# Gate and up with four of eight k-pairs by seven block products in chunks 1 to 9, and the third weight sum of a block by an adding DMA

## The chip, the cores and the metric

One core of one Trainium2 chip runs the whole kernel. The metric is device time in microseconds (us). Engines: PE is TensorE (matmul), DVE is VectorE, ACT is ScalarE, POOL is GpSimd, SP is SyncE, which here only issues loads.

## The reference

One decoder layer on 256 tokens of width 2048, all in float32: a SwiGLU feed-forward (FFN), a token mixer (SSD and attention), a second FFN, each with a residual and a layer norm. The change touches the two FFNs:

```python
def swiglu(x, w_gate, w_up, w_down):        # 2048 -> 5632 -> 2048
    return (jax.nn.silu(x @ w_gate) * (x @ w_up)) @ w_down
```

## The kernel before

**Products.** Every float32 operand is split into a high part (rounded to fp32r by an ACT copy) and a low part (DVE: value minus high). One product of a 128-row tile of activations with a 128x512 tile of weights is three matmuls: high by high, high by low, low by high. The activations (`a_hi`, `a_lo`, transposed, 16 k-tiles x 256 tokens) stay in SBUF, the weights stream.

**Slabs.** SP loads the weights in slabs of 128x2x512 (512 KB: two k-tiles, 512 columns) into a ring of `LAND` = 4 buffers `land`. ACT makes `w_hi` of a slab (L1309), DVE makes `w_lo` (L1728), both rings of `SPLIT` = 4. ACT starts slab n once PE has used slab n-4 (semaphore `used`), PE starts slab n when its low part is there (`rest`), and SP reloads a `land` buffer when DVE is through with it (`rest` too). Each engine runs its own list of instructions strictly in order.

**FFN stages.** Gate and up take 11 chunks of 512 hidden columns (`up1`, `up2`), 16 slabs a chunk; down takes 2 double columns of 44 slabs (`down1`, `down2`). A chunk's accumulators fill one half of PSUM (`acc` or `spare`, by turns). A plain pair of slabs is 8 products, 24 matmuls.

**Seven products.** In chunks 1 to 9 the two slabs of a k-pair (gate and up, slabs 2b and 2b+1) that is in `SEVEN` are taken as a 2x2 block product with 7 in place of 8 products (21 matmuls), and so are the five pairs `DOWN_SEVEN` in each half of down. It needs four sums of weight tiles, g0, g1 being the gate slab's k-tiles and u0, u1 the up slab's. DVE makes them in `block_sums` (L1926): u0+u1, g0+u0 (written over u0 in `land`), g0+u0+u1, and that plus g1. The block's up slab is split by ACT only after the second sum. Three of the sums are operands of their own and are split into `t_hi` and `t_lo` (ACT L1420 and L1422, DVE L1943 and L1946), which exist once: ACT may write them again when PE has finished with those of the block before (`t_used`). It also needs sums of activations, which are made once per FFN (`s_hi`, `s_lo`, one pair of buffers for each member of `SEVEN`; `mixed_of`, `mixed_low`).

**The order on DVE** is written out by hand in `up_seven`: besides the 16 splits it has, at slab 1, `collect` (shared sums of the chunk before, out of PSUM), at slab 3 `sum_chunk`, at slab 4 `product_summed`, at slab 6 `hidden_low`, and ahead of slab 2b of a member of `SEVEN` `block_sums`. In the FFN stages POOL has only two refills of `resid` and a few small operations for the layer norms.

Of the kernel before, what the change touches and what calls it, by code (L numbers as in the profile page):

```python
# [19 lines left out]
F32 = mybir.dt.float32  # L20
# [64 lines left out]
SEVEN = (2, 4, 6)  # L85
# [187 lines left out]
def build_decoder_layer(nc, x, positions, ffn1_w_gate, ffn1_w_up, ffn1_w_down, ln1_g, ln1_b, w_in, conv_w, conv_b,  # L273
# [20 lines left out]
    with ctx:  # L294
# [6 lines left out]

        resid = sb("resid", [P, TOK, D])
# [7 lines left out]
        def placed(name, shape, dt, at):  # L310
# [40 lines left out]
        sz = sb("sz", [P, TOK, W])  # L351
        bcT = sb("bcT", [P, 2, SEQ])
        b_tok = sb("b_tok", [P, P])
        cbm = sb("cbm", [P, TOK, P])
# [23 lines left out]
        t_hi = placed("t_hi", [P, 2, W], F32R, 36 * K)  # L378
        t_hi_four = placed("t_hi_four", [P, W], F32R, 40 * K)
        t_lo = placed("t_lo", [P, 2, W], F32R, 80 * K)  # L380
        t_lo_four = placed("t_lo_four", [P, W], F32R, 84 * K)
        d_s = [(placed(f"d_hi{k}", [P, 4, P], F32R, at * K), placed(f"d_lo{k}", [P, 4, P], F32R, (at + 2) * K))
               for k, at in enumerate((88, 92, 108, 112, 116))]
        d_t_hi = placed("d_t_hi", [P, 2, W], F32R, 96 * K)
        d_t_hi_four = placed("d_t_hi_four", [P, W], F32R, 100 * K)
        d_t_lo = placed("d_t_lo", [P, 2, W], F32R, 102 * K)
        d_t_lo_four = placed("d_t_lo_four", [P, W], F32R, 106 * K)
# [32 lines left out]
        sums = sem("sums")  # L420
        t_high = sem("t_high")
# [160 lines left out]
        def _(pool):  # L582
# [146 lines left out]
            keep_stream(TOK * NC_D)  # L729
            pool.wait_ge(kept_out, 2 * 16 * NC_D)  # L730
# [4 lines left out]
            pool.dma_start(resid[:, :, 0:2 * W], kept_view[:, :, 0:2 * W]).then_inc(resid_in, 16)  # L735
            pool.wait_ge(used, slab_no("down2", 1, 2 * DOWN_ORDER[1].index(7) + 1) + 1)
# [5 lines left out]
        def _(pe):  # L742
# [132 lines left out]
            def seven_products(n, slab_at, lg, lu, rows_of, mixed, t_set, own, aux, first, last, turned=None):  # L875
# [424 lines left out]
        def _(act):  # L1300
# [163 lines left out]
            def down(f):  # L1464
                for j in range(2):
                    for l, (p, c) in enumerate(DOWN_SLABS[j]):
# [9 lines left out]
                        if s in DOWN_SEVEN and c == 1:  # L1476
                            n = down_block(f, j, DOWN_SEVEN.index(s))
                            act.wait_ge(sums, n * 4 + 2)
                            split(f"down{f}", j, l)
# [242 lines left out]
        def _(dve):  # L1722
# [203 lines left out]
            def block_sums(phase, i, l, n):  # L1926
# [616 lines left out]
```

## Time and profile before

| | |
|---|---|
| median of 3 runs | 2670.63 us (2668.64 to 2671.52) |
| the profiled execution | 2668.99 us, span 2667.4 us |
| granted TensorE clock | 0.996 of full speed |
| PE busy | 2634.5 us, 99% |
| DVE busy | 2002.6 us, 75% |
| ACT busy | 1361.7 us, 51% |
| DMA | 513.96 MB, mean 193 GB/s |

The span runs from the first to the last instruction of one execution. Busy shares are means over stages: in the chunks with seven products DVE is far above its mean share. A matmul's row is longer (0.39 us) than the distance to the next matmul, since they are pipelined; the distance is what a matmul costs.

### The profile page before, as it was taken

How to read it: one execution, taken by the hardware profiler on the slowest of the kernel's cores; microseconds unless marked ns; L12 is line 12 of the kernel's file. 1: busy time of each engine (PE TensorE's matmuls, PEld its weight loads, DVE VectorE, ACT ScalarE, POOL GpSimd, SP SyncE). 2: the span in 40 equal slices, each digit the busy share in tenths (PEclk: the TensorE clock that was granted, in tenths of full speed). 3: DMA queues.
4: the chain of work that ended last, by engine and by line, in shares of the span. 5: the costliest groups of instructions: out<-in, count | busy, mean ns of one | idle time of the engine just before them, and what ended most of it. 6: DMA issues, size and time to landing. Idle time of an engine off the chain costs nothing.

```text
span 2667.4 us, 36687 instructions
## 1 busy us (share of the span) xinstructions
PE 2634.5 (99%) x12546; PEld 2188.8 (82%) x12546; DVE 2002.6 (75%) x2410; ACT 1361.7 (51%) x1678; POOL 130.0 (5%) x170
## 2 busy tenths in 40 slices
PE   8999999999999999999999999999999999999997
PEld 7888888888787788888888888888878888888886
DVE  6999997688666665677777765444689999977986
ACT  5555555455344454566555554444355555554553
POOL 1000000000000000211111100000000000000000
PEclk9999999999999999999999999999999999999999
DMA  6666566666655546665555565667666665666664
GB/s 224 204 191 209 185 205 204 214 200 204 189 171 147 156 150 197 206 181 179 177 177 177 179 183 165 190 190 247 200 190 204 190 211 186 205 202 229 210 208 171
DMA packets 286195, 513.96 MB, mean 193 GB/s; under 512 B 19648, under 2 KB 52592, under 8 KB 284048
## 3 DMA queue, kind: packets, MB, share of 16 engines
q1 hardware_dynamic: 279552, 485.03, 57.8%
q0 software_dynamic: 4880, 25.36, 2.6%
q10 hardware_dynamic: 1664, 2.26, 0.2%
q8 instruction: 61, 1.00, 0.2%
q14 instruction: 38, 0.31, 0.0%
HBM read 506.23 MB, written 6.36 MB: 192 GB/s over the span
## 4 chain that ended last, share of the span: by engine, by line
PE 95%; DVE 3%; ACT 1%; issue 0%; DMA 0%; POOL 0%; POOLq 0%; SPq 0%; ACTq 0%; DVEq 0%
PE acc L787 13%; PE acc L789 13%; PE acc L788 13%; PE acc L853 5%; PE acc L855 5%; PE acc L854 5%; PE acc L871 4%; PE acc L872 4%; PE acc L873 4%; PE spare L871 4%; PE spare L872 4%; PE spare L873 4%; PE spare L855 3%; PE spare L854 3%; PE spare L853 3%; PE spare L756 2%
## 5 line engine op out<-in xcount | busy, mean ns | idle before, releaser
L1728 DVE TENSOR_TENSOR w_lo<-land,w_hi 128x1024 fp32r<-128x1024 f32 (+1 forms) x956 | 1149.2, 1219 | 499.4 <-ACT w_hi L1309 490.6
L1309 ACT ACTIVATE w_hi<-land 128x1024 fp32r<-128x1024 f32 (+1 forms) x956 | 976.8, 1029 | 916.9 <-PE acc L789 328.0
L787 PE MATMUL acc<-w_hi,a_hi 128*128 128x512 f32 (+1 forms) x1184 | 451.2, 381 | 2.6 <-DVE a_lo L1775 1.8
L789 PE MATMUL acc<-w_hi,a_lo 128*128 128x512 f32 (+1 forms) x1184 | 435.8, 368 | 0.0
L788 PE MATMUL acc<-w_lo,a_hi 128*128 128x512 f32 (+1 forms) x1184 | 434.4, 367 | 0.0
L787 PEld LDWEIGHTS acc<-w_hi,a_hi 128*128 128x128 f32 x1184 | 223.9, 189 | 46.8 <-issue 9.2
L789 PEld LDWEIGHTS acc<-w_hi,a_lo 128*128 128x128 f32 x1184 | 223.6, 189 | 38.2
L788 PEld LDWEIGHTS acc<-w_lo,a_hi 128*128 128x128 f32 x1184 | 224.1, 189 | 37.4 <-issue 3.6
L853 PE MATMUL acc<-w_hi,a_hi 128*128 128x512 f32 x576 | 227.7, 395 | 2.0 <-DVE a_lo L1775 1.7
L855 PE MATMUL acc<-w_hi,a_lo 128*128 128x512 f32 x576 | 225.1, 391 | 0.0
L854 PE MATMUL acc<-w_lo,a_hi 128*128 128x512 f32 x576 | 225.0, 391 | 0.0
L853 PE MATMUL spare<-w_hi,a_hi 128*128 128x512 f32 x400 | 156.6, 391 | 0.0
L855 PE MATMUL spare<-w_hi,a_lo 128*128 128x512 f32 x400 | 155.8, 389 | 0.0
L854 PE MATMUL spare<-w_lo,a_hi 128*128 128x512 f32 x400 | 155.6, 389 | 0.0
L853 PEld LDWEIGHTS acc<-w_hi,a_hi 128*128 128x128 f32 x576 | 108.8, 189 | 25.4 <-DVE a_lo L1775 2.1
L855 PEld LDWEIGHTS acc<-w_hi,a_lo 128*128 128x128 f32 x576 | 108.6, 189 | 23.0
L854 PEld LDWEIGHTS acc<-w_lo,a_hi 128*128 128x128 f32 x576 | 108.9, 189 | 21.9
L871 PE MATMUL spare<-w_hi,g_hi 128*128 128x512 f32 x292 | 114.0, 390 | 0.7 <-DVE w_lo L1728 0.7
L873 PE MATMUL spare<-w_hi,g_lo 128*128 128x512 f32 x292 | 113.6, 389 | 0.0
L872 PE MATMUL spare<-w_lo,g_hi 128*128 128x512 f32 x292 | 113.6, 389 | 0.0
L871 PE MATMUL acc<-w_hi,g_hi 128*128 128x512 f32 x292 | 113.6, 389 | 0.0
L872 PE MATMUL acc<-w_lo,g_hi 128*128 128x512 f32 x292 | 113.6, 389 | 0.0
(388 smaller groups left out, 4233.1 us busy)
## 6 DMA issues: line engine op xcount, KB each, us to landing
land<-w_in SPq DMA_DIRECT2D x232, 512.0 KB, 3.9
land<-ffn_w_gate SPq DMA_DIRECT2D x176, 512.0 KB, 3.9
land<-ffn_w_up SPq DMA_DIRECT2D x176, 512.0 KB, 4.3
land<-ffn_w_down SPq DMA_DIRECT2D x176, 512.0 KB, 4.7
land<-w_ssd_o SPq DMA_DIRECT2D x64, 512.0 KB, 4.3
land<-w_in SPq DMA_DIRECT2D x132, 128.0 KB, 2.3
land<-w_attn_o SPq DMA_DIRECT2D x32, 512.0 KB, 4.1
land<-w_out SPq DMA_DIRECT2D x32, 512.0 KB, 4.4
```

What stands on the lines that cost most here:

```text
L756: return pe.transpose(spare[0:src.shape[-1], bank, at:at + rows], src, ident[0:rows, 0:rows])
L787: pe.matmul(to, rows_hi, hi, start=first, stop=False)
L788: pe.matmul(to, rows_hi, lo, start=False, stop=False)
L789: mm = pe.matmul(to, rows_lo, hi, start=False, stop=last)
L853: pe.matmul(to, rows_hi, hi, start=first and k == 0, stop=False)
L854: pe.matmul(to, rows_hi, lo, start=False, stop=False)
L855: mm = pe.matmul(to, rows_lo, hi, start=False, stop=last and k == 1)
L871: pe.matmul(to, rows[0], block[0], start=first, stop=False)
L872: pe.matmul(to, rows[0], block[1], start=False, stop=False)
L873: return pe.matmul(to, rows[1], block[0], start=False, stop=last)
L1309: act.activation(w_hi[:, l % SPLIT, 0:deep, 0:width], land[:, l % LAND, 0:deep, 0:width], ACT.Copy).then_inc(high, 1)
L1728: dve.tensor_tensor(w_lo[:, l % SPLIT, 0:deep, 0:width], land[:, l % LAND, 0:deep, 0:width], w_hi[:, l % SPLIT, 0:deep, 0:width].bitcast(F ...
```

## The change

1. `SEVEN` becomes (2, 4, 5, 6): one more k-pair of chunks 1 to 9 of both FFNs by 7 products. Pairs 4, 5 and 6 are neighbours. A fourth pair of buffers for the mixed activations and one more mixing per FFN come with it.
2. The sum u0+u1 is no longer made by DVE. After DVE's first sum (g0+u0, which no longer goes over u0), POOL issues a DMA that reads u1 again from HBM (128x512, 256 KB) and adds it onto u0 in `land`. ACT splits the block's up slab after that has landed (semaphore `third_added`, L1469). This holds for the blocks of down too.
3. The other three sums lie side by side in `t_sums` and are split by one ACT and one DVE instruction of 128x1536 (L1451, L1969) in place of two each.
4. Order: ACT splits the three sums before the up slab, DVE likewise. PE takes the three products that need `t_hi` in the middle of the block, behind the gate slab's, and those of the up slab last. `collect` waits for the last up slab in place of `t_used`.

```diff
-SEVEN = (2, 4, 6)
+SEVEN = (2, 4, 5, 6)
...
+            def add_third(slot, n, block):
+
+                pool.wait_ge(sums, n * 3 + 1)
+                pool.dma_start(land[:, slot, 0, :], block, accum_op=ALU.add).then_inc(third_added, 16)
...
                 three(own[:, 0, :], rows_of(1, 0), block(lg, 1)).then_inc(used, 1)
+                pe.wait_ge(t_rest, n + 1)
+                three(aux[:, 1, :], mixed_rows(1), t_block(0), first, last)
+                if turned is not None:
+                    pe.wait_ge(gt_out, turned)
+                three(aux[:, 3, :], mixed_rows(2), t_block(1), first, last)
+                three(own[:, 1, :], rows_of(1, 1), t_block(2)).then_inc(t_used, 1)
                 pe.wait_ge(rest, slab_at + 2)
                 three(own[:, 2, :], mixed_rows(3), block(lu, 1))
-                three(aux[:, 1, :], mixed_rows(1), block(lu, 0), first, last).then_inc(used, 1)
-                if turned is not None:
-                    pe.wait_ge(gt_out, turned)
-                pe.wait_ge(t_rest, n * 2 + 1)
-                three(aux[:, 2, :], mixed_rows(0), t_block(0), first, last)
-                three(aux[:, 3, :], mixed_rows(2), t_block(1), first, last)
-                pe.wait_ge(t_rest, n * 2 + 2)
-                three(own[:, 1, :], rows_of(1, 1), t_block(2)).then_inc(t_used, 1)
+                three(aux[:, 2, :], mixed_rows(0), block(lu, 0), first, last).then_inc(used, 1)
...
-                act.wait_ge(sums, n * 4 + 3)
+                act.wait_ge(sums, n * 3 + 3)
                 if not is_zero(n):
                     act.wait_ge(t_used, n)
-                act.activation(hi[:, :, :], sz[:, :, :], ACT.Copy).then_inc(t_high, 1)
-                act.wait_ge(sums, n * 4 + 4)
-                act.activation(hi_four[:, :], t_four, ACT.Copy).then_inc(t_high, 1)
+                act.activation(t_of[t_set][0][:, :, :], t_sums[:, :, :], ACT.Copy).then_inc(t_high, 1)
...
+                    n = seven_block(f, i, l // 2) if l // 2 in SEVEN else None
+                    if n is not None and l % 2 == 1:
+                        act.wait_ge(third_added, n * 16 + 16)
+                    split(f"up{f}", i, l)
+                    if n is not None and l % 2 == 0:
                         t_high_parts(n, "up")
...
-                dve.tensor_tensor(sz[:, 0, :], up[:, 0, :], up[:, 1, :], ALU.add).then_inc(sums, 1)
-                dve.wait_ge(sums, n * 4 + 1)
-                dve.tensor_tensor(up[:, 0, :], gate[:, 0, :], up[:, 0, :], ALU.add).then_inc(sums, 1)
-                dve.wait_ge(sums, n * 4 + 2)
-                dve.tensor_tensor(sz[:, 1, :], up[:, 0, :], up[:, 1, :], ALU.add).then_inc(sums, 1)
-                dve.wait_ge(sums, n * 4 + 3)
+                dve.tensor_tensor(sz[:, 0, :], gate[:, 0, :], up[:, 0, :], ALU.add).then_inc(sums, 1)
+                dve.wait_ge(sums, n * 3 + 1)
+                dve.tensor_tensor(sz[:, 1, :], sz[:, 0, :], up[:, 1, :], ALU.add).then_inc(sums, 1)
+                dve.wait_ge(sums, n * 3 + 2)
                 dve.tensor_tensor(t_four, sz[:, 1, :], gate[:, 1, :], ALU.add).then_inc(sums, 1)
...
-                    split(f"up{f}", i, l)
                     if l // 2 in SEVEN and l % 2 == 1:
                         t_low_parts(seven_block(f, i, l // 2), "up")
+                    split(f"up{f}", i, l)
```

The order on DVE in chunk 1, before, from the sums of pair 4 (slabs 8 and 9) to the first sum of pair 6; `w_lo` is a slab's split (x2: two in a row), `t_lo` and `t_lo_four` those of the sums:

```order
L1931 TENSOR_TENSOR sz<-land 128x512
L1933 TENSOR_TENSOR land<-land 128x512
L1935 TENSOR_TENSOR sz<-land 128x512
L1937 TENSOR_TENSOR bcT<-sz,land 128x512
L1728 TENSOR_TENSOR w_lo<-land,w_hi 128x1024 x2
L1943 TENSOR_TENSOR t_lo<-sz,t_hi 128x1024
L1946 TENSOR_TENSOR t_lo_four<-bcT,t_hi_four 128x512
L1728 TENSOR_TENSOR w_lo<-land,w_hi 128x1024 x2
L1931 TENSOR_TENSOR sz<-land 128x512
```

The same engine and place in the changed kernel, pairs 4 and 5:

```order
L1959 TENSOR_TENSOR t_sums<-land 128x512
L1961 TENSOR_TENSOR t_sums<-t_sums,land 128x512
L1963 TENSOR_TENSOR t_sums<-t_sums,land 128x512
L1756 TENSOR_TENSOR w_lo<-land,w_hi 128x1024
L1969 TENSOR_TENSOR t_lo<-t_sums,t_hi 128x1536
L1756 TENSOR_TENSOR w_lo<-land,w_hi 128x1024
L1959 TENSOR_TENSOR t_sums<-land 128x512
L1961 TENSOR_TENSOR t_sums<-t_sums,land 128x512
L1963 TENSOR_TENSOR t_sums<-t_sums,land 128x512
L1756 TENSOR_TENSOR w_lo<-land,w_hi 128x1024
L1969 TENSOR_TENSOR t_lo<-t_sums,t_hi 128x1536
L1756 TENSOR_TENSOR w_lo<-land,w_hi 128x1024
```

One sum fewer stands ahead of a block's splits, the split of the sums has moved ahead of the up slab's, and pair 5, which had two plain splits, repeats the whole sequence directly behind pair 4.

The order on PE in chunk 1, before: the second half of pair 4's block and the plain slab behind it. Only the first of each product's three matmuls stands here:

```order
L871 MATMUL spare<-w_hi,s_hi1_84 128x512 [waits rest]
...
L871 MATMUL acc<-w_hi,s_hi1_84 128x512
...
L871 MATMUL acc<-t_hi_89,s_hi1_84 128x512 [waits t_rest]
...
L871 MATMUL acc<-t_hi_89,s_hi1_84 128x512
...
L871 MATMUL spare<-t_hi_four_90,a_hi_49 128x512 [waits t_rest]
...
L853 MATMUL spare<-w_hi,a_hi_49 128x512 [waits rest]
```

The same engine in the changed kernel, from the last `t_hi` product of pair 4 to the first of pair 5:

```order
L904 MATMUL spare<-t_hi_91,a_hi_49 128x512
...
L904 MATMUL spare<-w_hi,s_hi1_84 128x512 [waits rest]
...
L904 MATMUL acc<-w_hi,s_hi1_84 128x512
...
L904 MATMUL acc<-w_hi,a_hi_49 128x512 [waits rest]
...
L904 MATMUL spare<-w_hi,a_hi_49 128x512
...
L904 MATMUL acc<-t_hi_91,s_hi2_85 128x512 [waits t_rest]
```

Between the last use of `t_hi` in one block and its first use in the next there are now four products, twelve matmuls. Before, a plain pair and the first four products of the next block lay between, 36 matmuls.

## Rows read from the trace of the kernel before

**Rows 1.** page, part 1: busy us (share of the span) xinstructions of each engine
```profile
PE 2634.5 (99%) x12546; PEld 2188.8 (82%) x12546; DVE 2002.6 (75%) x2410; ACT 1361.7 (51%) x1678; POOL 130.0 (5%) x170
```

**Rows 2.** windows, two of up 1 and one of down 1; us, busy of PE, PEld, DVE, ACT, POOL
```profile
84.00:126.00 42.00, 42.00 (x191) 34.86 (x190) 39.09 (x43) 23.81 (x26) 0.00 (x0) 1.00 0.60 192
126.00:168.00 42.00, 42.00 (x191) 34.88 (x190) 38.46 (x42) 23.83 (x26) 0.00 (x0) 1.00 0.63 198
511.00:604.00 93.00, 93.00 (x412) 77.01 (x411) 82.35 (x98) 47.66 (x51) 0.00 (x0) 1.00 0.62 202
```

**Rows 3.** timeline, PE: the first product of a block, and of the slab behind
```profile
154.66 0.39 PE L871 MATMUL acc<-w_hi,a_hi 128*128 128x512 f32 x1
...
159.42 0.39 PE L853 MATMUL spare<-w_hi,a_hi 128*128 128x512 f32 x1
```

**Rows 4.** timeline, DVE: pair 4 of one chunk; start us, us, instruction [idle before]
```profile
158.13 0.68 DVE L1931 TENSOR_TENSOR sz<-land 128x512 f32<-128x512 f32 x1
...
160.30 0.69 DVE L1937 TENSOR_TENSOR bcT<-sz,land 128x512 f32<-128x512 f32 x1
160.91 2.35 DVE L1728 TENSOR_TENSOR w_lo<-land,w_hi 128x1024 fp32r<-128x1024 f32 x2
163.18 1.22 DVE L1943 TENSOR_TENSOR t_lo<-sz,t_hi 128x1024 fp32r<-128x1024 f32 x1
164.32 0.69 DVE L1946 TENSOR_TENSOR t_lo_four<-bcT,t_hi_four 128x512 fp32r<-128x512 f32 x1
164.92 2.46 DVE L1728 TENSOR_TENSOR w_lo<-land,w_hi 128x1024 fp32r<-128x1024 f32 x2
167.65 0.69 DVE L1931 TENSOR_TENSOR sz<-land 128x512 f32<-128x512 f32 x1 [0.27 <-DMA land<-ffn_w_up]
```

**Rows 5.** timeline, DVE: the other work of a chunk
```profile
139.72 1.22 DVE L1954 TENSOR_TENSOR resid<-spare,resid 128x1024 f32<-128x1024 f32 x1
...
143.14 1.21 DVE L1870 TENSOR_TENSOR resid<-resid,acc 128x1024 f32<-128x1024 f32 x1
...
145.60 1.22 DVE L1728 TENSOR_TENSOR w_lo<-land,w_hi 128x1024 fp32r<-128x1024 f32 x1
146.74 1.22 DVE L1877 TENSOR_TENSOR resid<-resid 128x1024 f32<-128x1024 f32 x1
147.88 0.68 DVE L1931 TENSOR_TENSOR sz<-land 128x512 f32<-128x512 f32 x1
...
154.67 1.28 DVE L1885 SCALAR_TENSOR_TENSOR g_lo<-acc,g_hi 128x512 f32 x2
155.87 2.35 DVE L1728 TENSOR_TENSOR w_lo<-land,w_hi 128x1024 fp32r<-128x1024 f32 x2
...
180.65 0.69 DVE L1952 TENSOR_TENSOR resid<-resid,acc 128x512 f32<-128x512 f32 x1 [1.71 <-ACT resid L1427]
...
182.10 1.23 DVE L1954 TENSOR_TENSOR resid<-acc,resid 128x1024 f32<-128x1024 f32 x1
```

**Rows 6.** groups of instructions, up 1, ACT: busy us, mean ns | idle before
```profile
L1309 ACT ACTIVATE w_hi<-land 128x1024 fp32r<-128x1024 f32 x129 | 137.0, 1062 | 130.1 <-DVE land L1933 53.0 <-PE spare L855 35.6 <-PE acc L855 34.5
...
L1420 ACT ACTIVATE t_hi<-sz 128x1024 fp32r<-128x1024 f32 x24 | 25.1, 1044 | 0.0
...
L1422 ACT ACTIVATE t_hi_four<-bcT 128x512 fp32r<-128x512 f32 x24 | 14.8, 615 | 0.0
```

**Rows 7.** DMA issues: KB each, median us from issue to landing
```profile
land<-ffn_w_up SPq DMA_DIRECT2D x176, 512.0 KB, 4.3
...
kept<-resid POOLq DMA_DIRECT2D x8, 512.0 KB, 3.6
...
resid<-x POOLq DMA_DIRECT2D x2, 1024.0 KB, 8.1
...
out<-resid ACTq DMA_DIRECT2D x8, 256.0 KB, 2.0
...
par<-conv_w POOLq DMA_DIRECT2D x2, 48.0 KB, 5.5
```

More of the change, by code:

```diff
@@ L349, in build_decoder_layer @@
         state = placed("state", [P, W], F32, 94 * K)
[L351 to L354, printed above, removed]
+        t_sums = sb("t_sums", [P, 3, W])
+        sz = t_sums[:, 0:TOK, :]
+        t_four = t_sums[:, TOK, :]
+        bcT = t_four.rearrange("p (k n) -> p k n", k=2)
+        group_at = -(-nc.sbuf_base // 32) * 32
+        group = sb("group", [P, 4, P])
+        b_tok = group[:, 0, :]
+        cbm = group[:, 1:1 + TOK, :]
         ident = sb("ident", [P, P])
@@ L377, in build_decoder_layer @@
         s_lo = [placed(f"s_lo{k}", [P, 4, P], F32R, at * K) for k, at in enumerate((94, 86, 42))]
[L378 to L381, printed above, removed]
+        s_hi.append(placed("s_hi3", [P, 4, P], F32R, resid_at - at0 + 8 * W))
+        s_lo.append(placed("s_lo3", [P, 4, P], F32R, group_at - at0))
+        t_hi = placed("t_hi", [P, 3, W], F32R, 36 * K)
+        t_lo = placed("t_lo", [P, 3, W], F32R, 80 * K)
         d_s = [(placed(f"d_hi{k}", [P, 4, P], F32R, at * K), placed(f"d_lo{k}", [P, 4, P], F32R, (at + 2) * K))
                for k, at in enumerate((88, 92, 108, 112, 116))]
[L384 to L387, printed above, removed]
+        d_t_hi = placed("d_t_hi", [P, 3, W], F32R, 96 * K)
+        d_t_lo = placed("d_t_lo", [P, 3, W], F32R, 102 * K)
         d_parts = placed("d_parts", [P, 3, W], F32, 120 * K)
-        t_of = {"up": (t_hi, t_hi_four, t_lo, t_lo_four),
-                "down": (d_t_hi, d_t_hi_four, d_t_lo, d_t_lo_four)}
-        t_four = bcT[:, :, :].rearrange("p k n -> p (k n)")
+        t_of = {"up": (t_hi, t_lo), "down": (d_t_hi, d_t_lo)}
         q_one = resid[:, 0, 3 * W:4 * W]
@@ L420, in build_decoder_layer @@
         sums = sem("sums")
+        third_added = sem("third_added")
         t_high = sem("t_high")
@@ L651, in refill_late, with up_thirds, chunk, down_thirds @@
                 pool.dma_start(resid[:, :, 2 * W:], view[:, :, 2 * W:]).then_inc(resid_late_in, 16)
+            def add_third(slot, n, block):
+                pool.wait_ge(sums, n * 3 + 1)
+                pool.dma_start(land[:, slot, 0, :], block, accum_op=ALU.add).then_inc(third_added, 16)
+            def up_thirds(f):
+                def chunk(i):
+                    for b in SEVEN:
+                        add_third((2 * b + 1) % LAND, seven_block(f, i, b), ffn_w[f][1][:, 2 * b + 1, bass.ds(i * W, W)])
+                for i in range(1, ALONE + 1):
+                    chunk(i)
+                with pool.Fori(1, 1 + (NC_S - ALONE) // 2) as m:
+                    for k in range(2):
+                        chunk(m * 2 + (ALONE - 1 + k))
+            def down_thirds(f):
+                for j in range(2):
+                    for l, (p, c) in enumerate(DOWN_SLABS[j]):
+                        s = DOWN_ORDER[j][p]
+                        if s in DOWN_SEVEN and c == 1:
+                            at = (2 * j + 1) * W
+                            add_third(l % LAND, down_block(f, j, DOWN_SEVEN.index(s)),
+                                      ffn_w[f][2][:, 2 * s + 1, at:at + W])
+            up_thirds(1)
             refill_late(1, x_view)
@@ L655, in _ @@
             pool.dma_start(resid[:, :, 0:2 * W], x_view[:, :, 0:2 * W]).then_inc(resid_in, 16)
+            down_thirds(1)
             deviations(1)
@@ L729, in _ @@
             keep_stream(TOK * NC_D)
+            up_thirds(2)
             pool.wait_ge(kept_out, 2 * 16 * NC_D)
@@ L883, in t_block @@
                 def t_block(m):
-                    hi, hi_four, lo, lo_four = t_of[t_set]
-                    return (hi[:, m, :], lo[:, m, :]) if m < 2 else (hi_four[:, :], lo_four[:, :])
+                    hi, lo = t_of[t_set]
+                    return hi[:, m, :], lo[:, m, :]
                 pe.wait_ge(rest, slab_at + 1)
@@ L1457, in copy_one_down @@
             def copy_one_down(f, j):
-                act.wait_ge(t_used, down_block(f, j, len(DOWN_SEVEN) - 1) + 1)
+                last = 2 * DOWN_ORDER[j].index(DOWN_SEVEN[-1]) + 1
+                act.wait_ge(used, slab_no(f"down{f}", j, last) + 1)
                 if j == 1:
@@ L1475, in down @@
                             copy_one_down(f, 1)
[L1476 to L1479, printed above, removed]
+                        n = down_block(f, j, DOWN_SEVEN.index(s)) if s in DOWN_SEVEN else None
+                        if n is not None and c == 1:
+                            act.wait_ge(third_added, n * 16 + 16)
+                        split(f"down{f}", j, l)
+                        if n is not None and c == 0:
                             t_high_parts(n, "down")
-                        else:
-                            split(f"down{f}", j, l)
             ffn(1, "xT", None)
@@ L2080, in down @@
                             block_sums(phase, j, l, n)
-                        split(phase, j, l)
                         if n is not None and c == 1:
                             t_low_parts(n, "down")
+                        split(phase, j, l)
                 evacuate_down(f, 1, 0)
```

25 lines of the change are left out of this document (9 added, 16 removed).

## The prediction

> **What bounds the kernel now.** I read the page's busy times first: PE is busy for 99% of the span [rows 1], so a change pays only where PE gets less to do and isn't made to wait. Then the windows, because DVE's 75% is a mean: in chunks of `up1` with seven products PE is busy for all of 42.00 us and DVE for 38.5 to 39.1; in `down1` DVE is busy for 82.35 of 93.00 [rows 2]. So these chunks have two engines near their limit, PE at it and DVE some 3 us behind it. The timelines give prices. From the first product of a block to the slab behind it, 21 matmuls, are 159.42 - 154.66 = 4.76 us, 0.2267 us each [rows 3]. A chunk is 182.10 - 139.72 = 42.38 us (from `collect` to `collect`) [rows 5].
>
> **What DVE does in a chunk**, by the distance from start to start, which is what an instruction costs its engine. A split of a slab: (163.18 - 160.91)/2 = 1.135. Four sums: three at (160.30 - 158.13)/3 = 0.723 and a last one at 0.61, together 2.78; the splits of the sums 1.14 + 0.60 = 1.74 [rows 4]. `sum_chunk` 145.60 - 143.14 = 2.46, `product_summed` 1.14, `hidden_low` 155.87 - 154.67 = 1.20, `collect` 182.10 - 180.65 = 1.45 and one more of 1024 elements, 1.14 [rows 5]. Before: 16 x 1.135 + 2.46 + 1.14 + 1.20 + 2.59 = 25.55, and three blocks of 4.52, 39.1 us in all.
>
> **The change, part by part.**
>
> Saved on PE: one more pair by 21 in place of 24 matmuls, 3 x 0.2267 = 0.68 us a chunk; 9 chunks in each of 2 FFNs, 18 x 0.68 = 12.2 us. That is all there is to win: the reordering inside a block takes no matmul away.
>
> DVE after: a block has three sums, 2 x 0.723 + 0.61 = 2.06, and one split of 1536 elements. Of 512 elements this kind takes 0.69 us, of 1024 1.22 [rows 4], so 1536 take 1.75, and 1.14 + 0.53 = 1.67 from start to start. 3.73 a block, four blocks 14.9: 40.5 us of work in a chunk of 41.7. It fits, but only 1.2 us is left for waits.
>
> The new wait of DVE in each block. The split of the sums now stands ahead of the up slab's, so only the gate slab's split covers ACT's work on `t_hi`. ACT takes 0.615 us for 512 and 1.044 for 1024 elements [rows 6], so 1.47 for 1536. From the start of the third sum: it ends at 0.69, ACT runs from 0.73 to 2.20, DVE could go on at 2.24 (0.04 for a signal, as between 158.13 + 0.68 and the next sum) and is there at 0.61 + 1.135 = 1.75. It waits 0.5 us, four times a chunk, 2.0. A second wait: pair 4's sums need slab 9, whose load starts when slab 5 is split. From the end of such a split to the first sum that waited for its landing are 167.65 - (160.91 + 2.35) = 4.39 us [rows 4]. Between the two DVE now has only `hidden_low` and two splits (before, the split of the sums as well): slab 5's split starts, slab 9 is there 1.22 + 4.39 = 5.6 later, DVE is there at 1.14 + 1.20 + 2.27 = 4.6. 1.0 us. DVE-paced, a chunk is then 40.5 + 2.0 + 1.0 = 43.5 us, **1.1 more than now**, if the adding DMA is never late.
>
> The new wait of PE. `t_hi` and `t_lo` exist once. Let 0 be where PE has issued the last `t_hi` product of pair 4 (its result is there at 0.16, since a row is 0.39 long [rows 3]). ACT makes pair 5's `t_hi` from 0.20 to 1.67, DVE `t_lo` from 1.71 to 3.46. PE has only 12 matmuls in between, 2.72 us, and goes on at 3.50: **0.78 us** of waiting. Its nine matmuls end at 5.54, slab 11's six at 6.90. DVE, started at 1.71, meanwhile has the split of the sums (1.67), slab 11 (1.14), three sums (2.06) and slab 12's split (1.22 to its end): 7.8. PE waits **0.93**, and its six matmuls end at 9.19. ACT begins `t_hi` of pair 6 when the sums are there, at 6.69, DVE has `t_lo` at 9.95: PE waits **0.80**. 2.5 us a chunk, so a PE-paced chunk is 42.38 - 0.68 + 2.51 = 44.2 us, **1.8 more than now**. Pairs 2 and 4 are covered by a plain pair, as all are now. Behind pair 6 six plain slabs follow, in which DVE catches up.
>
> The adding DMA, which no row of this trace shows. Call A the time from POOL's issue to its landing. Counted from the first sum's start it is issued at 0.73 and landed at 0.73 + A; ACT splits the up slab (1.06 [rows 6]), and DVE can take it at 1.87 + A. DVE's own work brings it there at 2.06 + 1.135 + 0.5 + 1.67 = 5.4. So A is free up to 3.5 us. Above that each us costs DVE 4 us a chunk. With the 0.7 by which the PE-paced chunk is longer, the run grows from A = 3.7 on, by 18 x 4 = 72 us for each us. Bounds: 2.0 us, a transfer of the same 256 KB, from another queue with no loads beside it; 8.1 us, 1024 KB on POOL's queue beside the slabs [rows 7]. Between them, on POOL's queue, 512 KB took 3.6 and the smallest 5.5, and a slab of 512 KB takes 4.3 on SP's [rows 7]. The add fetches 256 KB and must also read the 256 KB that it adds to, so I count it as 512 KB and take the middle of 3.6 and 4.3, 3.9 us.
>
> The Trainium skill (DMA: Bandwidth & Descriptors, Anatomy of one DMA, SWDGE path) fits such a transfer by 2.0 us plus 1 us for each 436,000 bytes: an estimate of 2.6 us for 256 KB, by which the add would never be late and the sum would be that of the first rival. For 512 KB it gives 3.2, below the 3.6 of POOL's row [rows 7].
>
> Queues and neighbours. POOL has nothing else in these chunks; its refills come behind the last add, and the add's wait for a sum holds back nothing that another engine wants. The loads get 1 MB a chunk more beside 8 MB. The fourth mixing (some 2.3 us of DVE in chunk 0, twice) lies in a chunk with PE nearly full and six slabs to catch up; I count it at nothing, at most 5 us. Down: a block and the plain pair behind it are 45 matmuls, 10.2 us; DVE has 3.73 + 4 x 1.135 + 0.5 = 8.8. 1.4 us is spare, so down loses nothing until A = 4.9 and gains nothing, since its matmuls stay as many.
>
> **The sum.** With A = 3.9 a chunk is DVE-paced at 43.5 + 4 x 0.4 = 45.1 us, 2.7 more than 42.38; 18 chunks, 49 us. Against the profiled execution's own 2668.99 that is 2718 us. The median of the three runs is 1.6 us above that execution, which I leave inside the rounding.
>
> **The rivals.**
> - *The add is in time* (A up to 3.7, chance 0.33). PE's three waits remain: 18 x 1.83 = 33 us, 2702. For it: 2.0 us for 256 KB, 3.6 for twice that; against it: a slab of the same traffic takes 4.3.
> - *The add is slow by nature* (A above 5.5, 0.11). At 5.5 a chunk is 51.5, 18 x 9.1 = 164 us, and 20 blocks of down lose 0.6 each: 2845. At 8.1 it is 3084. For it: the smallest transfers of POOL took 5.5, and this one reads what it writes to.
> - *PE's wait isn't there* (faster, 0.09). If ACT and DVE had the three sums' splits ready within the 12 matmuls at pairs 5 and 6, PE would keep its 0.68 us a chunk: 2657. It decides at the place of the 0.78: the two splits and three signals would have to take 2.6 us, not 3.3. For it: only that no instruction of 1536 elements stands in the trace. Against it: two sizes of each do, and they lie on a line. Waits that come to 0.68 a chunk give 2669, no change (0.04).
>
> **How the numbers follow.** The forecast, an add of 3.7 to 5.5 us that makes DVE the pace, has 0.43: from 2702 to 2845, with 2718 where the nearest rows put it. The range from 2690 to 2840 takes in the first rival with some us less waiting than worked out, and leaves out the slow add (0.11) and the two cases without loss. A measurement here can tell about 0.2%, 5.3 us, from no change: slower by more 0.87, within it 0.04, faster 0.09.
>
> **What would show it.** In the changed kernel's chunks: PE idle at L904 for 0.8 us twice and 0.9 once, released by the split of the sums (L1969) and by a slab's split (L1756); DVE idle for 0.5 us ahead of L1969, released by ACT L1451; the add's row with its landing, and ACT's L1341 waiting for it, if A is above 3.5; a chunk of 44 to 45 us. No idle PE at pairs 5 and 6 would make the prediction wrong, and so would an A far from 4.

## The result, and the profile after

| | before | changed |
|---|---|---|
| median | 2670.57 us (4 runs, 2668.64 to 2671.52) | 2831.78 us (4 runs, 2828.56 to 2836.22) |
| profiled execution, span | 2667.4 us | 2826.9 us |
| a chunk of `up1` with seven products, `collect` to `collect`, mean of 8 | 42.39 us | 50.08 us |

The ratio is 1.0606, 95% interval 1.0587 to 1.0624: 161 us slower. I had forecast slower by 49, 2690 to 2840. The time lies inside that range, near its end, but the loss is 3.3 times the one that I forecast.

The page of the changed kernel: busy times, and the chain that ended last by engine and by line.

```profile
PE 2672.9 (95%) x12492; PEld 2167.7 (77%) x12492; DVE 2028.6 (72%) x2344; ACT 1369.1 (48%) x1624; POOL 209.2 (7%) x262
...
PE 53%; DMA 23%; DVE 13%; issue 6%; ACT 4%; POOLq 0%; DVEq 0%; POOL 0%; ACTq 0%; SPq 0%
DMA land<-ffn_w_up 16%; PE acc L820 13%; PE acc L822 12%; PE acc L821 12%; DMA land<-ffn_w_down 7%; DVE w_lo L1756 5%; ACT w_hi L1341 4%; DVE t_sums L1959 2%; PE spare L789 2%; PE acc L886 2%; PE acc L888 2%; PE acc L887 2%; PE spare L1242 1%; PE acc L904 1%; PE acc L905 1%
```

PE's share fell from 99% [rows 1] to 95%, and the chain now runs for 23% of the span through DMAs, nearly all of them `land<-ffn_w_up` and `land<-ffn_w_down`. Windows of the changed kernel, two in `up1` and one in `down1` (us, then busy of PE, PEld, DVE, ACT and POOL with counts, granted clock, DMA share, GB/s):

```profile
105.00:155.00 50.00, 44.06 (x190) 34.25 (x189) 41.01 (x41) 24.54 (x24) 3.47 (x4) 1.00 0.69 190
155.00:205.00 50.00, 42.81 (x185) 33.24 (x185) 39.94 (x40) 23.90 (x24) 3.49 (x4) 1.00 0.66 183
615.00:710.00 95.00, 91.54 (x393) 72.63 (x392) 70.19 (x69) 41.30 (x40) 5.11 (x6) 1.00 0.68 204
```

PE did 191 matmuls in 42 us before [rows 2] and does 185 to 190 in 50 us now, at the same granted clock. DVE is busy for 80 to 82%, less than the 92 to 93% of before [rows 2]: it has little more to do and waits for the rest. DVE's timeline at pair 4 (start us, us, instruction, idle before it and who ended that):

```profile
174.86 0.69 DVE L1959 TENSOR_TENSOR t_sums<-land 128x512 f32<-128x512 f32 x1 [0.23 <-DMA land<-ffn_w_up]
...
176.31 0.69 DVE L1963 TENSOR_TENSOR t_sums<-t_sums,land 128x512 f32<-128x512 f32 x1
176.92 1.22 DVE L1756 TENSOR_TENSOR w_lo<-land,w_hi 128x1024 fp32r<-128x1024 f32 x1
178.56 1.76 DVE L1969 TENSOR_TENSOR t_lo<-t_sums,t_hi 128x1536 fp32r<-128x1536 f32 x1 [0.42 <-ACT t_hi L1451]
182.26 1.23 DVE L1756 TENSOR_TENSOR w_lo<-land,w_hi 128x1024 fp32r<-128x1024 f32 x1 [1.95 <-ACT w_hi L1341]
183.41 0.68 DVE L1959 TENSOR_TENSOR t_sums<-land 128x512 f32<-128x512 f32 x1
```

The splits of a slab and the sums take what they took in [rows 4], the split of 1536 elements takes 1.76 us (1.75 worked out), and DVE waits 0.42 us for `t_hi` (0.5 worked out). The next row is the loss: the up slab's split at 182.26 comes after 1.95 us of idleness. DVE could have had it at 178.56 + 1.67 = 180.2. POOL's adds, and ACT:

```profile
176.18 0.88 POOL L658 DMA_DIRECT2D land<-ffn_w_up  x1 [10.78 <-DVE t_sums L1959]
184.72 0.87 POOL L658 DMA_DIRECT2D land<-ffn_w_up  x1 [7.67 <-DVE t_sums L1959]
```

```profile
177.03 1.49 ACT L1451 ACTIVATE t_hi<-t_sums 128x1536 fp32r<-128x1536 f32 x1 [3.32 <-DVE t_sums L1963]
181.17 2.01 ACT L1341 ACTIVATE w_hi<-land 128x1024 fp32r<-128x1024 f32 x2 [2.65 <-DMA land<-ffn_w_up]
185.58 1.48 ACT L1451 ACTIVATE t_hi<-t_sums 128x1536 fp32r<-128x1536 f32 x1 [2.40 <-DVE t_sums L1963]
189.80 2.00 ACT L1341 ACTIVATE w_hi<-land 128x1024 fp32r<-128x1024 f32 x2 [2.74 <-DMA land<-ffn_w_up]
```

The first sum of pair 4 ends at 174.86 + 0.69 = 175.55. POOL begins the DMA at 176.18, 0.63 us later, and ACT can split the up slab at 181.17, 4.99 us after that. In pair 5 it is 184.72 to 189.80, 5.08. DMA issues (KB each, median us from issue to landing):

```profile
land<-ffn_w_gate SPq DMA_DIRECT2D x176, 512.0 KB, 4.7
...
land<-ffn_w_up POOLq DMA_DIRECT2D x72, 256.0 KB, 4.6
...
land<-ffn_w_down POOLq DMA_DIRECT2D x20, 256.0 KB, 4.5
```

The add takes 4.6 us to land. The slabs of gate take 4.7, which had 3.9 before; those of up, which took 4.3 [rows 7], now take 3.8. Four of PE's waits at pairs 5 and 6:

```profile
186.74 0.50 PE L904 MATMUL acc<-w_hi,a_hi 128*128 128x512 f32 x1 [1.09 <-DVE w_lo L1756]
...
188.91 0.50 PE L904 MATMUL acc<-t_hi,s_hi 128*128 128x512 f32 x1 [0.52 <-DVE t_lo L1969]
...
192.18 0.50 PE L904 MATMUL spare<-w_hi,s_hi 128*128 128x512 f32 x1 [0.94 <-DVE w_lo L1756]
...
195.37 0.50 PE L904 MATMUL acc<-w_hi,a_hi 128*128 128x512 f32 x1 [1.53 <-DVE w_lo L1756]
```

One of these waits (188.91) is the `t_lo` wait that I had worked out; the others are for a slab's split. Over the chunks of `up1` (105 to 555 us) PE waits 16 times for `t_lo`, 8.2 us together, and 32 times for a slab's split, 29.7 us: it now waits mostly for what the late add holds up. A third wait comes once a chunk, in pair 2's block (8 times, 12.1 us): there PE waits for `hidden_low`, which DVE does behind the up slab's split, and so behind the add.

### The profile page after: what moved, and what is told of

Same layout as the page of the kernel before. It is cut to its first block, busy times and chain, and to the rows that moved or that the text cites. A ratio compares the mean times of both kernels' runs of the same rounds, so it can differ in the third digit from the quotient of the medians.

```text
span 2826.9 us, 36677 instructions
## 1 busy us (share of the span) xinstructions
PE 2672.9 (95%) x12492; PEld 2167.7 (77%) x12492; DVE 2028.6 (72%) x2344; ACT 1369.1 (48%) x1624; POOL 209.2 (7%) x262
## 3 DMA queue, kind: packets, MB, share of 16 engines
q10 hardware_dynamic: 1664, 2.26, 0.2%
## 4 chain that ended last, share of the span: by engine, by line
PE 53%; DMA 23%; DVE 13%; issue 6%; ACT 4%; POOLq 0%; DVEq 0%; POOL 0%; ACTq 0%; SPq 0%
DMA land<-ffn_w_up 16%; PE acc L820 13%; PE acc L822 12%; PE acc L821 12%; DMA land<-ffn_w_down 7%; DVE w_lo L1756 5%; ACT w_hi L1341 4%; DVE t_sums L1959 2%; PE spare L789 2%; PE acc L886 2%; PE acc L888 2%; PE acc L887 2%; PE spare L1242 1%; PE acc L904 1%; PE acc L905 1%
## 5 line engine op out<-in xcount | busy, mean ns | idle before, releaser
L822 PEld LDWEIGHTS acc<-w_hi,a_lo 128*128 128x128 f32 x1184 | 223.5, 189 | 38.3
L821 PEld LDWEIGHTS acc<-w_lo,a_hi 128*128 128x128 f32 x1184 | 224.1, 189 | 37.3 <-issue 3.6
L1451 ACT ACTIVATE t_hi<-t_sums 128x1536 fp32r<-128x1536 f32 x72 | 107.1, 1487 | 211.7 <-DVE t_sums L1963 205.3
L886 PE MATMUL acc<-w_hi,a_hi 128*128 128x512 f32 x512 | 203.0, 396 | 3.8 <-DVE w_lo L1756 2.2
L887 PE MATMUL acc<-w_lo,a_hi 128*128 128x512 f32 x512 | 200.2, 391 | 0.0
L1969 DVE TENSOR_TENSOR t_lo<-t_sums,t_hi 128x1536 fp32r<-128x1536 f32 x72 | 126.6, 1759 | 31.6 <-ACT t_hi L1451 31.6
L658 POOL DMA_DIRECT2D land<-ffn_w_up x72 | 62.4, 867 | 896.2 <-DVE t_sums L1959 871.1
L886 PE MATMUL spare<-w_hi,a_hi 128*128 128x512 f32 x320 | 125.5, 392 | 0.0
L888 PE MATMUL spare<-w_hi,a_lo 128*128 128x512 f32 x320 | 124.6, 389 | 0.0
L887 PE MATMUL spare<-w_lo,a_hi 128*128 128x512 f32 x320 | 124.6, 389 | 0.0
```

Of the source, the lines that this page charges most:

```text
L821: pe.matmul(to, rows_hi, lo, start=False, stop=False)
L822: mm = pe.matmul(to, rows_lo, hi, start=False, stop=last)
L886: pe.matmul(to, rows_hi, hi, start=first and k == 0, stop=False)
L887: pe.matmul(to, rows_hi, lo, start=False, stop=False)
L888: mm = pe.matmul(to, rows_lo, hi, start=False, stop=last and k == 1)
L1451: act.activation(t_of[t_set][0][:, :, :], t_sums[:, :, :], ACT.Copy).then_inc(t_high, 1)
```

## The experiments

Eleven kernels, each an edit of the changed one. "Chunk" is the mean of eight distances from `collect` to `collect` in `up1`. "Against before" is against the kernel before as it ran beside each experiment (2669.3 to 2669.7 us). "Down" is what the two down stages lost in the profiled execution, from the last `collect` of up to the end of DVE's slabs. "Rest" is what remains of the loss after 18 x (chunk - 42.39): mostly down, and the first chunk of each FFN. It takes `up1`'s chunk for both FFNs, and in some kernels that use GpSimd the chunks of `up2` are shorter (49.55 us in the changed one, 44.66 in e1, 45.62 in e6, 45.67 in e9). Counted with them the rest is 28, 26, 17 and 16 us in these four.

| kernel | pairs | third sum | order | median us | against before | chunk us | rest us | down us |
|---|---|---|---|---|---|---|---|---|
| changed | 4 | awaited add | new | 2831.8 | +161.2 | 50.08 | 23 | 26 |
| e1_three | 3 | awaited add | new | 2739.6 | +69.9 | 44.99 | 23 | 28 |
| e2_dvesum | 4 | DVE | new | 2724.3 | +54.6 | 44.69 | 13 | 11 |
| e3_three_dvesum | 3 | DVE | new | 2681.4 | +11.7 | 42.39 | 12 | 10 |
| e4_poolsum | 4 | GpSimd | new | 2777.7 | +108.0 | 47.12 | 23 | 23 |
| e5_late | 4 | add, issued 1.45 us later | new | 2966.5 | +297.2 | 56.34 | 46 | 50 |
| e6_plain | 4 | copy, no add | new | 2748.5 | +79.2 | 46.11 | 12 | 17 |
| e7_traffic | 3 | DVE, adds to nobody | new | 2692.7 | +23.4 | 42.59 | 20 | 23 |
| e8_parts | 4 | DVE | by pair | 2722.9 | +53.6 | 45.38 | 0 | -1 |
| e9_half | 4 | half an add | new | 2747.8 | +78.5 | 46.03 | 13 | 15 |
| e10_nosum | 4 | none | new | 2718.1 | +48.8 | 44.47 | 11 | 8 |
| e11_nosum_parts | 4 | none | by pair | 2658.9 | -10.4 | 41.70 | 2 | 0 |

**e1_three**: pair 5 is taken plainly again.

```diff
-SEVEN = (2, 4, 5, 6)
+SEVEN = (2, 4, 6)
```

> The changed kernel with pair 5 taken plainly again (three pairs of seven products, as before), all else as changed: adding DMA, one split of 1536, new order. Theory (the late add paces the FFN chunks through VectorE): an add takes 0.6 us to start and 4.6 to land, 5.2 from the end of the first sum; three blocks a chunk each make VectorE wait 1.7 us and more, so a chunk is 44.3 to 46.5 us in place of 42.4 and the kernel is 40 to 80 us slower than before. Rival (the single t_hi/t_lo buffer between neighbouring pairs is what costs): no pairs are neighbours here, so it is within 10 us of before.

Ratio 1.0256 (1.0235 to 1.0276). With no neighbours in the chunk 70 us are still lost, so the add costs by itself.

**e2_dvesum**: DVE makes u0+u1, after the other three sums; no adding DMA.

```diff
...
-                        act.wait_ge(third_added, n * 16 + 16)
+                        act.wait_ge(sums, n * 4 + 4)
...
                 dve.tensor_tensor(t_four, sz[:, 1, :], gate[:, 1, :], ALU.add).then_inc(sums, 1)
+                dve.wait_ge(sums, n * 4 + 3)
+                dve.tensor_tensor(up[:, 0, :], up[:, 0, :], up[:, 1, :], ALU.add).then_inc(sums, 1)
...
```

> The changed kernel with four pairs, but the third weight sum made by VectorE again (in place, as the fourth of four sums; no adding DMA). Theory: TensorE's waits at the neighbouring pairs and VectorE's full chunk remain, 44 to 45 us a chunk: 30 to 45 us slower than before, and 115 to 130 us faster than the changed kernel. Rival (the add is everything, four pairs would win): 12 us faster than before.

Ratio 1.0205 (1.0188 to 1.0222), 107.5 us faster than the changed kernel. The chunk of 44.69 is where the theory had it; the total is 10 us above its range, and 11 are lost in down, which the theory left out.

**e3_three_dvesum**: both edits together.

> Three pairs and the third sum by VectorE, so that only the joined split of 1536 and the new order inside a block are left of the change. Theory: TensorE stays the bound, 0 us from before (within 5). Rival (the new order itself costs, since VectorE waits 0.4 us in each block for ACT's split of the sums): 5 to 30 us slower.

Ratio 1.0042 (1.0025 to 1.0059). The theory holds for the chunks, 42.39 as before, and not for the kernel: the new order costs 11.7 us, all outside them and 10 of them in down. The rival had the size, but not the place. With e1 the four kernels make a sum: order 11.7, pair 5 with the sum by DVE 42.9, the add 58.2 with three pairs and 107.5 with four.

**e4_poolsum**: GpSimd makes the sum.

```diff
-                pool.dma_start(land[:, slot, 0, :], block, accum_op=ALU.add).then_inc(third_added, 16)
+                pool.tensor_tensor(land[:, slot, 0, :], land[:, slot, 0, :], land[:, slot, 1, :], ALU.add
+                                   ).then_inc(third_added, 1)
...
```

> The changed kernel with four pairs, the third sum made by a GpSimd tensor_tensor of 128x512 in land in place of the adding DMA; ACT waits for it as it did for the DMA. A GpSimd instruction of that size takes 1.04 us in the SSD stage, so it is done long before ACT wants the up slab. Theory: only TensorE's waits at the neighbouring pairs remain, about 44.4 us a chunk: 30 to 40 us slower than before. Rival (VectorE and GpSimd hinder each other when both read SBUF): VectorE's rows of 1.22 us get longer where GpSimd runs, and it is over 60 us slower.

Ratio 1.0407 (1.0389 to 1.0424). The rival had the size, 108 us, but not the rows: DVE's splits of 1.22 us stay as they were, and one of its sums gets longer. Groups of instructions of this kernel, from 150 to 420 us (busy us, mean ns | idle before):

```profile
L658 POOL TENSOR_TENSOR land<-land 128x512 f32<-128x512 f32 x23 | 41.3, 1795 | 234.9 <-DVE t_sums L1960 234.9
...
L1964 DVE TENSOR_TENSOR t_sums<-t_sums,land 128x512 f32<-128x512 f32 x23 | 38.3, 1664 | 0.8
...
L1962 DVE TENSOR_TENSOR t_sums<-t_sums,land 128x512 f32<-128x512 f32 x23 | 15.9, 692 | 0.8
```

The third DVE sum (L1964), which runs beside GpSimd's, takes 1664 ns, and GpSimd's own takes 1795 where 1.04 us was the time of one of this size in the SSD stage. The second DVE sum (L1962, 692 ns) is no longer than before, although it starts within 0.1 us of GpSimd's row (177.40 and 177.44 in one block); rows of GpSimd are rough, and I did not settle why only the third one pays. Four times 0.97 us is 3.9 a chunk, and 43.5 + 3.9 = 47.4 (measured 47.12). The Trainium skill (SBUF — State Buffer, Who interferes with whom) has the rule: a DVE instruction with two SBUF inputs contends with a GpSimd instruction that reads SBUF. The trace agrees: 0.97 us more on DVE, 0.75 on GpSimd. So GpSimd's engine was no cheap place for a sum beside a busy DVE.

**e5_late**: the add is issued after the third sum.

```diff
-                pool.wait_ge(sums, n * 3 + 1)
+                pool.wait_ge(sums, n * 3 + 3)
```

> The changed kernel, but GpSimd issues the adding DMA after the third sum in place of the first, 1.45 us later (two sums at 0.72); nothing else moves. Theory (VectorE is paced by the add's landing, 4 times a chunk): a chunk grows by 4 x 1.45 = 5.8 us, from 49.8 to 55.6, and the kernel by 18 x 5.8 = 104 us up there plus at most 20 x 1.45 = 29 us in down: 105 to 135 us slower than the changed kernel. Rival (the add costs through the DMA traffic it makes, not through the wait): no slower than the changed kernel, within 10 us.

Ratio 1.1114 (1.1095 to 1.1132), 134.7 us slower than the changed kernel. The chunk grew by 6.26 us, 4.3 for each us of delay, where the theory had 4. Some of the difference may be TensorE's clock: in this run the granted clock was 0.87 to 0.96 over the stretches of 56 us from 108 to 556 us, where the changed kernel had 1.00, and the two chunks with 0.87 and 0.89 took 57.1 and 56.8 us, most of the others 55.8 to 56.1. Down lost 24 us more than in the changed kernel: at 6.6 us from sum to landing it is past its own spare time too.

**e6_plain**: the same DMA without the addition. The operand is u1 in place of u0+u1.

```diff
-                pool.dma_start(land[:, slot, 0, :], block, accum_op=ALU.add).then_inc(third_added, 16)
+                pool.dma_start(land[:, slot, 0, :], block).then_inc(third_added, 16)
```

> The changed kernel with the same 256 KB DMA from GpSimd's queue, without the addition: the tile u1 is copied over u0, so the output is not the reference's. It prices the addition itself. Theory: reading what it adds to is a second stream, so that without it the landing falls by the 0.4 to 1 us that I put on it, from 4.6 to about 3.8, and the kernel is 30 to 70 us faster than the changed one. Rival: fixed times of GpSimd's queue (0.6 us to start, the rest to land) make nearly all of it, and the kernel is the same within 15 us.

Ratio 1.0293 (1.0276 to 1.0310), 83 us faster than the changed kernel. Its DMA issues:

```profile
land<-ffn_w_up POOLq DMA_DIRECT2D x72, 256.0 KB, 3.7
```

0.9 us less to land, 4.0 us less of chunk. The theory had the direction and too small a size: 83 us, where it allowed 70.

**e9_half**: the add takes 256 of the 512 columns, so the sum is half made.

```diff
-                pool.dma_start(land[:, slot, 0, :], block, accum_op=ALU.add).then_inc(third_added, 16)
+                pool.dma_start(land[:, slot, 0, 0:W // 2], block[:, 0:W // 2], accum_op=ALU.add).then_inc(third_added, 16)
```

> The changed kernel, but the adding DMA takes only the first 256 of 512 columns (128 KB), so the sum is half made and the output is not the reference's. It tells size from fixed time. Theory (the landing is mostly fixed time: 4.6 us for 256 KB on GpSimd's queue, 5.5 for 48 KB at the start): landing falls by 0.5 us or less, 0 to 36 us faster than the changed kernel. Rival (bytes beside the slabs' traffic make it): landing falls by 1 us or more, over 60 us faster.

Ratio 1.0297 (1.0280 to 1.0314), 84 us faster than the changed kernel. Its DMA issues:

```profile
land<-ffn_w_up POOLq DMA_DIRECT2D x72, 128.0 KB, 3.6
```

My theory here was wrong and the rival right: half the bytes land 1.0 us earlier. Adding 128 KB (3.6 us) and copying 256 KB (3.7 us) take nearly the same.

**e7_traffic**: e3 with the same adds issued by GpSimd onto a scratch tile, and no engine of the computation waiting for them.

```diff
...
-                pool.wait_ge(sums, n * 3 + 1)
-                pool.dma_start(land[:, slot, 0, :], block, accum_op=ALU.add).then_inc(third_added, 16)
+                pool.wait_ge(sums, n * 4 + 1)
+                if not is_zero(n):
+                    pool.wait_ge(third_added, n * 16)
+                pool.dma_start(group[:, :, :].rearrange("p a n -> p (a n)"), block, accum_op=ALU.add
+                               ).then_inc(third_added, 16)
...
```

> Three pairs and the third sum by VectorE (the kernel that was 11.7 us slower than before), and GpSimd issues the same adding DMAs after the first sum, onto a scratch tile of 2 KB a partition for which no engine of the computation waits. It prices the traffic alone: 74 adds of 256 KB beside the slabs. Theory (the wait is the cost, not the traffic): within 8 us of the kernel without them, so 10 to 20 us slower than before. Rival (the adds slow down the slabs' loads and so VectorE): 30 us slower than before or more, as a good part of the 70 us of three pairs with the awaited add.

Ratio 1.0084 (1.0067 to 1.0101), 11.7 us above e3: more than the 8 that I allowed, far less than the 58.2 of the awaited add. The chunks grew by 0.2 us at most, 3 in all; down lost 23 us where e3 lost 10 (profiled executions). DVE's waits for the slabs' landing from 440 to 705 us, which is mostly `down1` (us in total, times, longest), before, in e3 and in e7:

```profile
DVE sz L1931 <- DMA land<-ffn_w_down: 2.4, 5, 0.7
```

```profile
DVE t_sums L1955 <- DMA land<-ffn_w_down: 13.2, 8, 2.9
```

```profile
DVE t_sums L1964 <- DMA land<-ffn_w_down: 22.6, 9, 4.0
```

**e10_nosum**: nobody makes the sum u0+u1; the product takes u0 alone.

```diff
...
-                        act.wait_ge(third_added, n * 16 + 16)
+                        act.wait_ge(sums, n * 3 + 1)
...
```

(The same in down, and GpSimd's calls of the add are gone.)

> The changed kernel without the sum u0+u1: no adding DMA, nobody makes the sum, ACT splits the up slab without a wait for it, so that product has the wrong operand and the output is not the reference's. This is the first rival of the prediction in pure form, an add that is never late. Theory: TensorE waits 0.8, 0.9 and 0.8 us at the neighbouring pairs, a chunk is 44.2 us, the kernel 33 us slower than before, some more with what down loses by the order (10 us, as with three pairs). Rival (the waits at the neighbours aren't there once VectorE has the time): 12 us faster than before, plus 10 of down.

Ratio 1.0183 (1.0166 to 1.0200). The theory's sum was 33 + 10, measured 48.8, and the chunk is 44.47 against 44.2. PE's waits over 270 us, some six chunks (us in total, times, longest):

```profile
PE spare L900 <- DVE t_lo L1965: 3.7, 6, 0.7
PE acc L900 <- DVE t_lo L1965: 3.7, 6, 0.7
PE spare L900 <- DVE w_lo L1752: 1.8, 3, 0.6
PE acc L900 <- DVE w_lo L1752: 1.8, 3, 0.6
```

Two waits for `t_lo` and one for a slab in each chunk, 0.6 us each, and nothing else. That idle time is 1.8 us a chunk, of the 2.8 by which the chunk is longer than e11's. A wait costs more than its idle time, as the starts show:

```profile
226.03 0.39 PE L902 MATMUL spare<-w_hi,s_lo 128*128 128x512 f32 x1
227.03 0.50 PE L900 MATMUL spare<-w_hi,a_hi 128*128 128x512 f32 x1 [0.61 <-DVE w_lo L1752]
227.36 0.39 PE L901 MATMUL spare<-w_lo,a_hi 128*128 128x512 f32 x1
```

The distance into the wait is 1.00 us in place of 0.227 and the one behind it 0.33: 0.88 us for 0.61 of idleness. The other two waits of this chunk, at 222.70 and 229.21, cost 0.99 and 0.81 in the same way, 2.7 together of the 2.8.

**e11_nosum_parts**: e10 with the parts of a block in an order that depends on the pair (g: the gate slab's products, t: those with `t_hi`, u: the up slab's); ACT and DVE split the up slab first.

```diff
+UP_PARTS = {2: "gtu", 4: "tgu", 5: "gtu", 6: "gut"}
...
+                    split(f"up{f}", i, l)
                     if l // 2 in SEVEN and l % 2 == 1:
                         t_low_parts(seven_block(f, i, l // 2), "up")
-                    split(f"up{f}", i, l)
...
```

> As the kernel without the sum u0+u1 (output not the reference's), but the order inside the blocks is chosen so that the single t_hi/t_lo buffer has time between neighbours: pair 4 takes its three t_hi products first, pair 5 in the middle, pair 6 last, 18 matmuls (4.1 us) between uses in place of 12 (2.7 us); ACT and VectorE split the up slab before the sums, as before the change, in up and in down. Theory: TensorE's waits vanish, a chunk is 41.7 to 41.9 us, the kernel 8 to 12 us faster than before. Rival (VectorE's load of four pairs is what makes TensorE wait, whatever the order): about as slow as the one with the order of the change, 30 to 45 us slower than before.

Ratio 0.9961 (0.9947 to 0.9975). Windows:

```profile
142.00:184.00 42.00, 42.00 (x191) 34.87 (x190) 40.61 (x41) 25.45 (x25) 0.00 (x0) 1.00 0.62 203
184.00:226.00 42.00, 42.00 (x191) 34.85 (x190) 40.91 (x41) 24.87 (x24) 0.00 (x0) 1.00 0.61 201
```

PE is busy for all of 42.00 us again and a chunk takes 41.70, which is 42.39 less 0.69: the three matmuls saved, at last. The same work in another order is 59 us faster than e10: 18 x 2.77 = 50 in the chunks, 9 in the rest, nearly all of it in down. The edit changed two things, the order of the parts on PE and that of the splits on ACT and DVE; I did not separate them.

**e8_parts**: e11's order, and DVE makes the sum. A complete kernel.

> Four pairs, the order with 18 matmuls between uses of t_hi, up slab split before the sums (the kernel without the sum that was 10.4 us faster than before), and now with the sum u0+u1 made by VectorE as the fourth of four: a complete kernel. Theory (VectorE's budget: 40.5 us without that sum, of a 41.8 us chunk): 4 x 0.72 more is 43.4 us, VectorE paces the chunk at 43.4 to 44.9, 18 to 45 us slower than before. Rival (the waits at the neighbours were all that four pairs cost): at least as fast as before.

Ratio 1.0201 (1.0183 to 1.0218). The chunk is 45.38, half a us above the theory's range. DVE at pairs 5 and 6:

```profile
218.11 0.69 DVE L1959 TENSOR_TENSOR t_sums<-land 128x512 f32<-128x512 f32 x1
...
220.90 2.51 DVE L1756 TENSOR_TENSOR w_lo<-land,w_hi 128x1024 fp32r<-128x1024 f32 x2
223.57 1.76 DVE L1971 TENSOR_TENSOR t_lo<-t_sums,t_hi 128x1536 fp32r<-128x1536 f32 x1 [0.16 <-ACT t_hi L1452]
225.53 0.69 DVE L1959 TENSOR_TENSOR t_sums<-land 128x512 f32<-128x512 f32 x1 [0.20 <-DVE t_lo L1971]
```

7.42 us from one block's sums to the next, where its work is 2.78 + 2.27 + 1.67 = 6.7: the last sum before the up slab's split now holds up ACT, and through it both splits. But even without that a chunk would be 43.4. This is what decides against four pairs: with the sum, DVE has more to do than a chunk of 42.39 holds. No version that I ran computes the reference in less time than the kernel before. An add that starts earlier, on a copy of u0 in a buffer of its own, was not tried.

## Why the prediction was wrong, step by step

**The saving on PE** was right: 0.68 us a chunk, and e11 shows 0.69.

**DVE's work and its wait for `t_hi`** were right: 0.41 to 0.42 us of waiting for 0.5. DVE's wait for slab 9 was too large: 1.0 us a chunk worked out, 0.4 measured (8 waits, 3.5 us, in `up1`). With both, the 43.5 us that a chunk should take with an add in time are some 0.9 too many.

**PE's waits at neighbouring pairs** were right: 2.5 us a chunk worked out, 2.35 measured in e10 (from start to start), and 0.3 more for the slower start behind each, so 44.47 - 41.70 = 2.8 between e10 and e11. The first rival, the add in time, was forecast at 2702; e10 is that case at 2718, of which 8 us were lost in down.

**The step that failed is the size of A**, "the middle of 3.6 and 4.3, 3.9 us", and with it the 0.04 us for a signal ahead of POOL's issue. The landing takes 4.6 us, and POOL begins 0.63 us after the sum that it waits for: 5.2 us from the sum, where I had 3.94. The rule around it holds. Above 3.5 us each us should cost 4 us a chunk: 43.5 + 4 x (5.2 - 3.5) = 50.3, measured 50.08; e6 with 0.9 us less gives 46.11; e5 with 1.45 us more gives 56.34. With the right size the sum would have been 18 x 7.9 = 143 us for the chunks; measured are 9 x 7.69 in `up1` and 9 x 7.16 in `up2`, 134. The agreement is in part luck, since the 43.5 is 0.9 too high and other waits in the chunk make that up. The slope is the firmer finding: 4.3 to 4.4 us a chunk for each us of path, from 4.3 to 6.6 us.

The 0.63 could have been read. In the trace before, POOL's refill waits for `sum_chunk`:

```profile
439.85 1.21 DVE L1870 TENSOR_TENSOR resid<-resid,spare 128x1024 f32<-128x1024 f32 x1
...
441.63 0.73 POOL L651 DMA_DIRECT2D resid<-x  x1 [431.20 <-DVE resid L1870]
```

The DVE row ends at 441.06 and POOL begins at 441.63, 0.57 us later. The signal was read from DVE to DVE, and this path ends at another engine. For the landing, I took the 3.6 us of `kept<-resid` as the price of 512 KB on POOL's queue. The equivalence that I used held at the one size tried, 128 KB added for 256 KB copied (e9 and e6). The row that I compared with did not: a plain copy of half its bytes, 256 KB, took 3.7 us in e6. Traffic does not explain that, since `kept<-resid` also ran beside slabs (DMA share 0.64 from 720 to 735 us, with 0.60 to 0.63 in the chunks [rows 2]). It is a store to HBM and the add a load, but no run separates the two, so why it lands sooner stays open. The nearer rows were the slabs' own, which are loads of 512 KB: 3.9 us for gate, 4.3 for up and 4.7 for down in the kernel before. The fit of the Trainium skill (DMA: Bandwidth & Descriptors, Anatomy of one DMA) gives an estimate of 2.6 us for 256 KB; the trace does not agree, since even the plain copy of e6 took 3.7 beside the slabs.

**Down** was forecast to lose nothing up to A = 4.9 and lost 26 us, counted as nothing in the sum. The runs show three parts.

- *The new order*, 8 to 11 us in down: e2, e3 and e10 lose 11, 10 and 8, while e8 and e11, with the old one, lose nothing. It is lost in `down2` (8.5 to 10.2 us); `down1` loses 0 to 2, though DVE's waits for landings there grew from 2.4 to 13.2. So those waits are mostly covered, and I had read them as the loss. PE in e3 idles for 0.6 us in all of `down1` and for 5.0 in `down2`, most of it in one place near the end:

```profile
2625.06 0.80 PE L900 MATMUL acc<-w_hi,g_hi 128*128 128x512 f32 x1 [3.48 <-DVE w_lo L1752]
```

There a slab lands late (ACT waits 5.3 us for it, while GpSimd loads `last_rows`, 2 MB), and DVE has the shared sums of `collect_down` ahead of the next four splits. e11 has no such wait of PE. Which part of the new order makes it, I did not test.

- *The adds' traffic*: e7, where nobody waits for the adds, loses 23 us in down, 13 more than e3, and `down1` then loses 12.
- *The wait for the add*, small in the changed kernel (26 against 23) and large in e5: 24 us more for 1.45 us of delay in 20 blocks, 29 at most. By my own threshold, with the path of 5.2 us in place of 4.9, it would have been 20 x 0.3 = 6.

**The rival "no wait at the neighbours"** (faster, 0.09) was wrong for this order and shows that order mattered: in e11, with 18 matmuls between uses in place of 12, the waits are gone.

## What to carry to other kernels

A DMA that stands between two engines is priced by its whole path, from the end of the work that it waits for to the start of the work that waits for it, in the traffic where it will run; when it sits in every block of a stage that is already full, each us of it above what the engines have to spare counted once per block here. Offloading 0.72 us of an engine's work onto a path of 5.2 us pays only where it can be issued that much ahead of its use. And an operand buffer that exists once needs its refill time (here 3.3 us) between the last use in one block and the first in the next: look at the order of uses before adding buffers, since 18 in place of 12 matmuls were enough here while DVE had time for the splits (e11; in e8, with one sum more on DVE, waits for `t_lo` came back).

## What the runs showed of the hardware

- An adding DMA of 256 KB on GpSimd's queue takes 0.87 us to issue and 4.6 to land; a plain one 0.54 and 3.7; an adding one of 128 KB 0.87 and 3.6 (medians, beside the stream of slabs). Adding 256 KB with three blocks a chunk took 4.3 (e1) and 4.2 (e7).
- GpSimd began a DMA 0.57 to 0.69 us after the DVE instruction that released it had ended (before, changed, e5, e6, e9; 0.70 to 0.79 in e7); DVE and ACT took 0.04.
- In e4 a `tensor_tensor` of 128x512 with both inputs in SBUF took 1.66 us on DVE in place of 0.69 beside one on GpSimd, and GpSimd's 1.80 in place of 1.04.
- In e10 a PE wait of 0.5 to 0.7 us idle cost 0.8 to 1.0 us from start to start.
